# The stick-breaking product with the values: four stationary blocks of weights with 64 value columns streamed, and outputs turned back

## The chip, the cores and the metric

The kernel runs on one core of a Trainium2 chip. The metric is device time in microseconds of one execution, as the median of several runs. One profiled execution gives the trace from which rows are read here. PE is TensorE's matmuls, PEld its loads of the stationary operand, DVE VectorE, ACT ScalarE, POOL GpSimd, SP the engine that issues most DMAs.

## What is computed

One layer of a hybrid trunk on 1040 tokens (16 meta tokens and 1024 inputs) of width 1024. The normed input is projected; eight heads of 64 go through an RWKV-7 scan, eight through stick-breaking attention; both are joined and projected, and an FFN of width 4096 follows. All is float32. The attention is what the change touches:

```python
def stick_breaking_group(q, k, v, out_gain):
    for q0, q1 in bounds:
        z = jnp.einsum('bhqd,bhkd->bhqk', qb, kb) * scale
        mask = s_idx[None, :] < t_idx[:, None]
        log_beta = jax.nn.log_sigmoid(z)
        log_1m = jnp.where(mask, log_beta - z, 0.0)
        log_a = log_beta + lax.cumsum(log_1m, axis=3, reverse=True) - log_1m
        A = jnp.where(mask, jnp.exp(log_a), 0.0)
        outs.append(jnp.einsum('bhqk,bhkd->bhqd', A, vb))
    o = jnp.concatenate(outs, axis=2)
    o = o * lax.rsqrt(jnp.mean(jnp.square(o), axis=-1, keepdims=True) + RMS_EPS)
```

## The kernel before

The kernel is a row of stages, each a block in which every engine has its own program and engines meet by semaphores: the norm and turning of the input, the input projection with the preparation of the scan, the mixing stage (`stage_mix`), the head norms, the output projection, and the FFN. The change lies in `stage_mix` alone, which runs from about 389 to 919 us.

`stage_mix` computes the scan and the attention side by side. The scan works in 17 chunks of 64 tokens, all four head pairs at once, in 64x64 products (`each`, `crossed`, `doubled`, `three`), of which each waits for a copy or a sum by ACT or DVE of the product before. A chunk is cut into 8 steps of a front and 8 of a rear; a lap does the front of one chunk beside the rear of the chunk before, and there are 18 laps.

The attention ("sticks") is a pipeline over tasks. A task is one pair `i` (of 4), one head `h` of it, one group `g` of 512 queries and one block `b` of 128 keys: 112 tasks, of which the ones at the diagonal are 128, 256 or 384 queries wide and the other 64 are 512 wide. Scores and probabilities lie with keys on partitions and queries along the free axis. `sb_ticks` writes the tasks in a row, one to a tick, with three `Turn` ticks for each pair between them, in which PE transposes blocks of values (`vt`) and ACT copies them to `v`. A task is spread over eight ticks. At its tick PE computes the scores `zb` from `ks`, `qh` and `ql`; one tick later ACT copies them to `z` and DVE clamps them to `w`; then come exponential and logarithm on ACT, a maximum on DVE, and a split into `wsh` and `wsl` on POOL. Four ticks later PE multiplies by the triangle `tri` into `cb` (the running sum), DVE forms the exponent in `a` (L1121), five ticks later PE adds the other triangle `rest` to `cb`, which it may do only when DVE has read `cb`, and ACT makes `a` to weights (L1017). Six ticks later PE multiplies with the values into the PSUM bank `ob` (L1290); after the last key block of a unit ACT copies the head's 64 rows of `ob` to `o_sb` (L999, named `mixed_o` in rows).

In the product of L1290 the values of both heads of the pair, 128 columns, are the stationary operand, and `a` moves, up to 512 columns; half of the 128 output rows belong to the other head and are not used. `o_sb` so receives channels on partitions and tokens along the free axis, which is how the later stages read it. All operands of this product are plain float32; of each such matmul the trace has two load rows and two matmul rows. The products with `tri_r`, `rest_r`, `qh` and `ql` are in a rounded type (fp32r) and have one row each.

`program` sets how both are mixed: it walks through 18 x 8 places of the scan and after each gives out quarter ticks of the sticks, so many that they are evenly dealt: 4 x (124 + 7 + 1) = 528 quarters over 144 places. On PE the quarters of a tick are: scores or transposes, `rest`, `tri`, values. Each engine executes its list strictly in this order.

## Time and profile before

| | us |
|---|---|
| median of three runs | 1801.07 (1801.05 to 1801.92) |
| the profiled execution's own time | 1802.92 |
| its span, first to last instruction | 1801.0 |
| mixing stage, 389 to 919 us of the span | 530.2 |
| PE busy in it | 498.1 |

A row of a timeline is start in us from the span's start, length in us, engine, line, operation, output and inputs by the program's names (first the operand that moves, then the stationary one), sizes, and how many instructions are merged into it. In brackets stands idle time of the engine before it and who ended it. A matmul's length is from its start until its result stands, so matmuls in a row overlap: of several merged ones, the length of all less the length of one, divided by their number less one, is how far apart they start. For loads of the stationary operand the same holds.

### The profile page before, as it was taken

What the parts mean: (1) busy time and instruction counts of PE and PEld (TensorE: products, weight loads), DVE (VectorE), ACT (ScalarE), POOL (GpSimd) and SP (SyncE); (2) the same over time, 40 slices, a digit from 0 to 9 for tenths busy, and PEclk for the clock granted to TensorE, in tenths of its full rate; (3) what the DMA queues carried; (4) which work ended last, traced back from release to release, by engine and by line L of the source; (5) the groups of instructions that cost most, each with busy time, mean ns of one, the idle gap of its engine ahead of it and who ended that gap; (6) DMA issues with size and microseconds to landing.
All of it is one profiled execution on the core that took longest, in us unless ns stands there. A gap on an engine that the chain in (4) does not pass through costs nothing. (4 is left out here: it accounts for less than half of the span.)

```text
span 1801.0 us, 36214 instructions
## 1 busy us (share of the span) xinstructions
PE 1671.0 (93%) x14676; PEld 1389.2 (77%) x14676; DVE 825.3 (46%) x1125; ACT 698.6 (39%) x1222; POOL 508.5 (28%) x523
## 2 busy tenths in 40 slices
PE   4999999969999998999983987999999999999998
PEld 4999999957777776777742876888888888888886
DVE  5132432426555556555565443444444444444436
ACT  5253443426566565666571443122212211221112
POOL 6332532404434434344452433111111111111110
PEclk7999999979999999999996998999999999999999
DMA  3235266283202213110022213111111111111104
GB/s 140 109 121 183 97 204 208 93 208 93 65 25 72 53 48 77 26 40 23 23 94 82 93 71 124 64 47 47 47 47 50 54 47 47 47 47 47 48 22 164
DMA packets 79386, 143.84 MB, mean 80 GB/s; under 512 B 15505, under 2 KB 51345, under 8 KB 79265
## 3 DMA queue, kind: packets, MB, share of 16 engines
q1 hardware_dynamic: 75520, 128.26, 23.1%
q10 hardware_dynamic: 3744, 13.85, 1.9%
q8 instruction: 91, 1.49, 0.3%
q14 instruction: 31, 0.25, 0.0%
HBM read 104.51 MB, written 37.57 MB: 79 GB/s over the span
## 5 line engine op out<-in xcount | busy, mean ns | idle before, releaser
L1749 POOL TENSOR_TENSOR ffn_ul<-ffn_relu,ffn_uh 128x512 fp32r<-128x512 f32 x64 | 82.9, 1296 | 576.5 <-ACT ffn_uh L1721 576.5
L1778 DVE TENSOR_TENSOR all_acc<-all_acc,ffn_down 128x512 f32<-128x512 f32 x240 | 161.0, 684 | 122.0 <-PE ffn_down L1825 121.4
L618 PE MATMUL inproj_acc<-xn_xh,inproj_wh 128*128 128x346 f32 (+1 forms) x624 | 207.5, 333 | 8.4 <-DVE inproj_wl L539 8.4
L1817 PE MATMUL ffn_up<-all_mh,ffn_wuh 128*128 128x512 f32 x512 | 200.3, 391 | 11.9 <-DVE ffn_wul L1761 11.9
L618 PE MATMUL inproj_acc<-xn_xh,inproj_wl 128*128 128x346 f32 (+1 forms) x624 | 201.2, 322 | 0.0
L618 PE MATMUL inproj_acc<-xn_xl,inproj_wh 128*128 128x346 f32 (+1 forms) x624 | 201.0, 322 | 0.0
L1817 PE MATMUL ffn_up<-all_ml,ffn_wuh 128*128 128x512 f32 x512 | 200.1, 391 | 0.0
L1817 PE MATMUL ffn_up<-all_mh,ffn_wul 128*128 128x512 f32 x512 | 200.0, 391 | 0.0
L1825 PE MATMUL ffn_down<-ffn_wdh,ffn_uh 128*128 128x512 f32 x512 | 199.8, 390 | 0.0
L1825 PE MATMUL ffn_down<-ffn_wdh,ffn_ul 128*128 128x512 f32 x512 | 199.4, 389 | 0.0
L1825 PE MATMUL ffn_down<-ffn_wdl,ffn_uh 128*128 128x512 f32 x512 | 199.2, 389 | 0.0
L1769 DVE TENSOR_TENSOR ffn_relu<-ffn_relu 128x512 f32<-128x512 f32 x64 | 44.3, 692 | 219.9 <-ACT ffn_relu L1719 219.9
L1713 ACT ACTIVATE ffn_wdh<-ffn_raw_d 128x1024 fp32r<-128x1024 f32 x32 | 32.2, 1052 | 266.1 <-PE ffn_down L1825 265.2
L618 PEld LDWEIGHTS inproj_acc<-xn_xh,inproj_wh 128*128 128x128 f32 x624 | 117.9, 189 | 12.1 <-ACT inproj_wh L472 8.8
L1817 PEld LDWEIGHTS ffn_up<-all_mh,ffn_wuh 128*128 128x128 f32 x512 | 96.7, 189 | 32.5 <-DVE ffn_wul L1761 12.3
L618 PEld LDWEIGHTS inproj_acc<-xn_xl,inproj_wh 128*128 128x128 f32 x624 | 118.0, 189 | 3.3 <-issue 1.9
L618 PEld LDWEIGHTS inproj_acc<-xn_xh,inproj_wl 128*128 128x128 f32 x624 | 118.0, 189 | 0.0
L1719 ACT ACTIVATE ffn_relu<-ffn_up 128x512 f32<-128x512 f32 x64 | 38.3, 599 | 203.9 <-PE ffn_up L1817 203.9
L912 POOL TENSOR_TENSOR mix_wsl<-mix_w,mix_wsh 128x512 fp32r<-128x512 f32 (+1 forms) x96 | 113.3, 1180 | 8.1
L1825 PEld LDWEIGHTS ffn_down<-ffn_wdh,ffn_uh 128*128 128x128 f32 x512 | 96.1, 188 | 22.1 <-DVE all_acc L1778 2.6
L1817 PEld LDWEIGHTS ffn_up<-all_mh,ffn_wul 128*128 128x128 f32 x512 | 96.7, 189 | 20.3
L1817 PEld LDWEIGHTS ffn_up<-all_ml,ffn_wuh 128*128 128x128 f32 x512 | 96.7, 189 | 20.0
(250 smaller groups left out, 3460.4 us busy)
## 6 DMA issues: line engine op xcount, KB each, us to landing
ffn_raw_u<-in_w_up SPq DMA_DIRECT2D x32, 512.0 KB, 3.5
ffn_raw_d<-in_w_down SPq DMA_DIRECT2D x32, 512.0 KB, 4.3
xn_raw<-in_w_in SPq DMA_DIRECT2D x28, 512.0 KB, 4.5
p_scratch<-inproj_out ACTq DMA_DIRECT2D x26, 520.0 KB, 2.7
chunk_scratch<-inproj_fields SPq DMA_DIRECT2D x4, 2720.0 KB, 9.2
mix_swp<-chunk_scratch SPq DMA_DIRECT2D x68, 128.0 KB, 3.6
inproj_rkv<-p_scratch SPq DMA_DIRECT2D x14, 520.0 KB, 4.5
mix_fld<-chunk_scratch SPq DMA_DIRECT2D x17, 256.0 KB, 3.0
```

The source lines that it names most:

```text
L618: last = pe.matmul(acc[g][:, 0:size], w[s][:, kt, :], xx[:, kt, col:col + size], start=(kt == 0 and j == 0), stop=(kt == KD - 1 and j == 2))
L912: pool.tensor_tensor(low, part, high.bitcast(F32), ALU.subtract).then_inc(soft_low.sem, 1)
L1713: act.activation(wdh[s][:, f, :], raw_d[f][:, :], ACT.Copy).then_inc(wd_high.sem, 1)
L1719: act.activation(relu[j % 2][:, :], ups[j][:, :], ACT.Relu).then_inc(relu_done.sem, 1)
L1749: pool.tensor_tensor(ul[s][:, f, cols], relu[j % 2][:, :], uh[s][:, f, cols].bitcast(F32), ALU.subtract).then_inc(u_low.sem, 1)
L1769: dve.tensor_tensor(relu[j % 2][:, :], relu[j % 2][:, :], relu[j % 2][:, :], ALU.mult).then_inc(squared.sem, 1)
L1778: dve.tensor_tensor(part, part, downs[o % 4][:, :], ALU.add).then_inc(added.sem, 1)
L1817: last = pe.matmul(ups[j][:, :], w[f][:, k, :], xx[:, k, cols], start=(k == 0 and jj == 0), stop=(k == KD - 1 and jj == 2))
L1825: last = pe.matmul(downs[o % 4][:, :], u[s][:, f, t * P:(t + 1) * P], w[s][:, f, g * 512:g * 512 + 512], start=(first and f == 0 and jj == ...
```

## The change

The product with the values exchanges its operands. `a` is now stationary, one 128x128 block at a time (128 keys by 128 queries), and the head's 64 value columns move. A 512-wide task takes four such products, a 384-wide one three, and so on: 352 in all instead of 112. Their outputs have queries on partitions: `ob[:, j*64:(j+1)*64]` holds query block `j`. The output copy on ACT takes 256 columns instead of 512 (in blocks of 64, written with a stride so that both heads of a pair stand beside each other in `o_sb`), on all 128 partitions instead of 64.

Since later stages want channels on partitions, a new kind of tick, `Back`, does four 128x128 transposes from `o_sb` into a score bank `zb` on PE, and ACT copies the bank back over the same part of `o_sb`. There are eight, one for each pair and group. Six stand among the tasks of the next pair (before its 6th and its 11th task), two at the end with empty ticks before them, which take the place of the seven ticks of run-out. The row of ticks becomes 139 long, and 4 x 140 = 560 quarters are dealt over the same 144 places.

```diff
+BACK_BEFORE = {5: 1, 10: 0}
...
+                    if n in BACK_BEFORE and i:
+                        ticks.append(Back(i - 1, BACK_BEFORE[n]))
                     ticks.append(Task(i, h, g, b))
                     n += 1
-    return ticks
+    return ticks + [None] * 3 + [Back(PAIRS - 1, 1)] + [None] * 4 + [Back(PAIRS - 1, 0)]
...
-            quarters = 4 * (N + SB_LAG + 1)
+            quarters = 4 * (N + 1)
...
+                    if is_back(t):
+                        z_done.wait(act, t)
+                        act.activation(o_sb[:, at(t).i, at(t).g * SBW:(at(t).g + 1) * SBW], zb[t % 2][:, :], ACT.Copy).then_inc(z_copied.sem, 1)
                     yield
...
-                        act.activation(o_sb[half, i, g * SBW:(g + 1) * SBW], ob[half, :], ACT.Copy).then_inc(o_copied.sem, 1)
+                        act.activation(o_sb[:, i, g * SBW:(g + 1) * SBW].rearrange("p (j n) -> p j n", n=P)[:, :, half],
+                                       ob[:, 0:SBW // 2].rearrange("p (j n) -> p j n", n=HD), ACT.Copy).then_inc(o_copied.sem, 1)
...
+                    if is_back(t):
+                        i, g = at(t).i, at(t).g
+                        o_copied.wait(pe, outputs(i, g))
+                        for j in range(SBW // P):
+                            last = pe.transpose(zb[t % 2][:, j * P:(j + 1) * P],
+                                                o_sb[:, i, g * SBW + j * P:g * SBW + (j + 1) * P], ident[:, :])
                         last.then_inc(z_done.sem, 1)
...
-                        pe.matmul(ob[:, off:], v[i % 2][:, b, :], a[t % 3][:, off:], start=first, stop=at(t).last,
-                                  skip_group_check=True).then_inc(pv_done.sem, 1)
+                        for j in range(off // P, SBW // P):
+                            last = pe.matmul(ob[:, j * HD:(j + 1) * HD], a[t % 3][:, j * P:(j + 1) * P], v[i % 2][:, b, at(t).half],
+                                             start=(first and j == off // P), stop=at(t).last, skip_group_check=True)
+                        last.then_inc(pv_done.sem, 1)
```

Since the quarters are dealt anew, instructions move against the scan's steps on every engine. Two places on PE show it. In the names a number is the buffer; `mix_bank` products are the scan's.

The first place is the task with `wsh1` early in the stage, between its product with `tri` and its product with `rest`. Before:

```order
L1244 MATMUL mix_cb<-mix_wsh1,mix_tri_r 128x512
L1245 MATMUL mix_cb<-mix_wsl1,mix_tri_r 128x512
L1136 MATMUL mix_bank<-mix_zi8,mix_xx8 64x64 x8
L1136 MATMUL mix_bank<-mix_xx8,mix_zi8 64x64 x8
L1290 MATMUL mix_ob<-mix_a1,mix_v0 128x512
L1259 MATMUL mix_zb0<-mix_qh,mix_ks 128x384
L1259 MATMUL mix_zb0<-mix_ql,mix_ks 128x384
L1244 MATMUL mix_cb<-mix_wsh1,mix_rest_r 128x512
```

and now, on the same engine at the same task:

```order
L1261 MATMUL mix_cb<-mix_wsh1,mix_tri_r 128x512
L1262 MATMUL mix_cb<-mix_wsl1,mix_tri_r 128x512
L1315 MATMUL mix_ob<-mix_v0,mix_a1 128x64 x4
L1276 MATMUL mix_zb0<-mix_qh,mix_ks 128x384
L1276 MATMUL mix_zb0<-mix_ql,mix_ks 128x384
L1261 MATMUL mix_cb<-mix_wsh1,mix_rest_r 128x512
L1262 MATMUL mix_cb<-mix_wsl1,mix_rest_r 128x512
L1153 MATMUL mix_bank<-mix_zi8,mix_xx8 64x64 x8
```

The scan's doubling step, which stood between `tri` and `rest`, stands behind `rest` now. Stretches of `tri`, values, scores and `rest` with no scan step inside are 12 in the order before and 19 in the new one.

The second place is PE's last lap, from the last `tri` on. Before:

```order
L1244 MATMUL mix_cb<-mix_wsh3,mix_tri_r 128x512
L1245 MATMUL mix_cb<-mix_wsl3,mix_tri_r 128x512
L1290 MATMUL mix_ob<-mix_a1,mix_v1 128x384
L1136 MATMUL mix_bank<-mix_fv0,mix_xt 64x128 x8
L1290 MATMUL mix_ob<-mix_a2,mix_v1 128x512
L1136 MATMUL mix_bank<-mix_nb0,mix_wu 64x128 x8
L1290 MATMUL mix_ob<-mix_a0,mix_v1 128x512
L1232 MATMUL mix_bank<-mix_wu,mix_nb0 64x64 x2
```

and now:

```order
L1261 MATMUL mix_cb<-mix_wsh1,mix_tri_r 128x512
L1262 MATMUL mix_cb<-mix_wsl1,mix_tri_r 128x512
L1315 MATMUL mix_ob<-mix_v1,mix_a1 128x64 x3
L1153 MATMUL mix_bank<-mix_xx32,mix_nb0 64x64 x8
L1315 MATMUL mix_ob<-mix_v1,mix_a2 128x64 x4
L1153 MATMUL mix_bank<-mix_xx32,mix_zi32 64x64 x8
L1315 MATMUL mix_ob<-mix_v1,mix_a0 128x64 x4
L1153 MATMUL mix_bank<-mix_fv0,mix_xt 64x128 x8
L1153 MATMUL mix_bank<-mix_nb0,mix_wu 64x128 x8
L1249 MATMUL mix_bank<-mix_wu,mix_nb0 64x64 x2
```

The last two products with the values moved in front of the scan's last three steps; behind the last scan product now stand the four transposes of the last `Back`.

## Rows read from the trace of the kernel before

**Rows 1.** The page: busy us of each engine, share of the span, instructions.

```profile
PE 1671.0 (93%) x14676; PEld 1389.2 (77%) x14676; DVE 825.3 (46%) x1125; ACT 698.6 (39%) x1222; POOL 508.5 (28%) x523
```

**Rows 2.** Stretches: length, busy us of PE, PEld, DVE, ACT, POOL; clock; DMA.

```profile
389.00:919.20 530.20, 498.14 (x9027) 387.32 (x9023) 293.80 (x556) 316.45 (x645) 207.99 (x320) 0.99 0.22 51
389.00:407.20 18.20, 14.87 (x259) 11.79 (x255) 7.29 (x14) 7.41 (x16) 0.35 (x1) 0.76 0.76 149
407.20:919.20 512.00, 483.27 (x8770) 375.53 (x8769) 286.52 (x542) 309.04 (x631) 207.63 (x319) 1.00 0.20 48
```

**Rows 3.** TensorE in order of time: matmuls and loads, merged and single.

```profile
576.67 1.02 PE L1290 MATMUL mix_ob<-mix_a,mix_v 128*128 128x512 f32 x2
...
559.55 0.59 PE L1290 MATMUL mix_ob<-mix_a,mix_v 128*128 128x512 f32 x1
...
576.35 0.30 PEld L1246 LDWEIGHTS mix_cb<-mix_w,mix_tri 128*128 128x128 f32 x2 [0.17 <-issue]
...
576.35 0.19 PEld L1246 LDWEIGHTS mix_cb<-mix_w,mix_tri 128*128 128x128 f32 x1 [0.17 <-issue]
...
905.12 0.38 PE L1290 MATMUL mix_ob<-mix_a,mix_v 128*128 128x128 f32 x2
...
577.77 0.27 PE L1246 MATMUL mix_cb<-mix_w,mix_rest 128*128 128x128 f32 x1
```

**Rows 4.** Waits in the stage: who for whom, us in total, times, longest.

```profile
PEld mix_cb L1244 <- DVE mix_a L1121: 29.3, 33, 2.0
...
PE mix_ob L1290 <- ACT mixed_o L999: 2.1, 5, 0.6
```

**Rows 5.** Transposes in order of time, ns min/median/max, and stretches with clock.

```profile
6.74 1.03 PE L167 MATMUL pre_tp<-all_ident,pre_xs 16*128 16x16 f32 x8 [6.74 <-DVE pre_xs L146]
...
10.70 2.34 PE L167 MATMUL pre_tp<-all_ident,pre_xs 128*128 128x128 f32 x10
...
1047.72 1.04 PE L1604 MATMUL oproj_tp<-all_ident,oproj_t 128*128 128x128 f32 x8
...
L167 PE MATMUL pre_tp<-all_ident,pre_xs x72: 262/421/477, 6.7 to 30.1; 128*128 128x128 f32 x64, 16*128 16x16 f32 x8
...
L1604 PE MATMUL oproj_tp<-all_ident,oproj_t x64: 270/273/477, 1000.2 to 1080.1; 128*128 128x128 f32 x64
...
20.19:22.16 1.97, 1.97 (x8) 1.57 (x8) 1.97 (x2) 1.89 (x5) 1.97 (x1) 0.50 0.00 0
1047.72:1048.80 1.08, 1.08 (x10) 1.06 (x9) 0.00 (x0) 0.89 (x1) 1.08 (x1) 1.00 0.00 0
```

**Rows 6.** Loads: ns min/median/max of a line; busy us and mean ns.

```profile
L1290 PEld LDWEIGHTS mix_ob<-mix_a,mix_v x224: 186/188/193, 416.3 to 914.1; 128*128 128x128 f32 x112
...
L1604 PEld LDWEIGHTS oproj_tp<-all_ident,oproj_t x64: 138/141/231, 1000.0 to 1079.8; 128*128 128x128 f32 x64
...
L1136 PEld LDWEIGHTS mix_bank<-mix_xx,mix_zi 64*64 64x64 f32 x1360 | 46.0, 136 | 0.3 <-issue 0.3
```

**Rows 7.** ACT's groups in the stage: count, busy us, mean ns, idle before.

```profile
L936 ACT ACTIVATE mix_nb<-mix_bank 128x512 f32<-128x512 f32 x17 | 10.1, 595 | 11.7 <-PE mix_bank L1145 11.6
...
L999 ACT ACTIVATE mixed_o<-mix_ob 64x512 f32<-64x512 f32 x16 | 9.4, 588 | 0.7 <-PE mix_ob L1290 0.5
...
L965 ACT ACTIVATE mixed_y<-mix_bank 128x256 f32<-128x256 f32 x17 | 6.5, 384 | 53.7 <-PE mix_bank L1232 53.7
```

**Rows 8.** The last lap in order of time: ACT, DVE, scan loads.

```profile
912.07 0.60 ACT L961 ACTIVATE mix_wu<-mix_bank 128x512 f32<-128x512 f32 x1 [1.90 <-PE mix_bank L1136]
...
918.55 0.59 ACT L999 ACTIVATE mixed_o<-mix_ob 64x512 f32<-64x512 f32 x1
...
914.14 0.69 DVE L1078 TENSOR_TENSOR mix_qm<-mix_bank,mix_fld 128x512 f32<-128x512 f32 x1 [3.06 <-PE mix_bank L1136]
...
913.00 0.85 PEld L1136 LDWEIGHTS mix_bank<-mix_nb,mix_wu 64*64 64x64 f32 x16 [0.76 <-ACT mix_wu L961]
...
915.08 0.20 PEld L1232 LDWEIGHTS mix_bank<-mix_wu,mix_nb 64*64 64x64 f32 x4 [0.76 <-DVE mix_qm L1078]
```

More of the change, by code:

```diff
@@ L693, in __init__ @@
         self.i, self.part = i, part
+class Back:
+    def __init__(self, i, g):
+        self.i, self.g = i, g
 def sb_ticks():
@@ L733, in stage_mix @@
     is_turn = lambda t: isinstance(at(t), Turn)
+    is_back = lambda t: isinstance(at(t), Back)
     task_ticks = [t for t in range(N) if is_task(t)]
@@ L736, in stage_mix @@
     last_ticks = [t for t in task_ticks if ticks[t].last]
+    back_at = {(ticks[t].i, ticks[t].g): t for t in range(N) if is_back(t)}
+    outputs = lambda i, g: max(t for t in last_ticks if (ticks[t].i, ticks[t].g) == (i, g))
     of_head = {(i, h): [t for t in task_ticks if (ticks[t].i, ticks[t].h) == (i, h)] for i in range(PAIRS) for h in range(2)}
@@ L801, in stage_mix @@
         split_no = lambda i, h: 2 * i + h
-        z_done, z_copied = (Marks(m.sem(name), range(N)) for name in ("z_done", "z_copied"))
+        z_done, z_copied = (Marks(m.sem(name), [t for t in range(N) if ticks[t]]) for name in ("z_done", "z_copied"))
         (clamped, exp_done, ln_done, soft, soft_high, soft_low, tri_done, exponent, rest_done, weights, pv_done) = (
@@ L893, in before_diagonal @@
                                    pattern=[[1, P]], channel_multiplier=-1).then_inc(marks.sem, 1)
-            for now in range(N + SB_LAG):
+            for now in range(N):
                 t = now - 5
@@ L979, in sticks @@
                 high_k(0, 0)
-                for now in range(N + SB_LAG + 1):
+                for now in range(N + 1):
                     t = now - 1
@@ L1096, in sticks @@
                 low_k(0, 0)
-                for now in range(N + SB_LAG + 1):
+                for now in range(N + 1):
                     t = now - 1
@@ L1248, in sticks @@
             def sticks():
-                for now in range(N + SB_LAG + 1):
+                for now in range(N + 1):
                     t = now
```

1 line of the change is left out of this document (added).

## The prediction

> **What bounds the kernel now.** I read the page first (busy shares, then the slices), then the mixing stage as one window, then who waits there for whom, and last single instructions of TensorE in order of time. The page gives TensorE (PE) 1671.0 of 1801.0 us [rows 1], and the change touches only the mixing stage, 389 to 919 us. There PE is busy 498.1 of 530.2 us, while DVE has 293.8, ACT 316.5 and GpSimd (POOL) 208.0 [rows 2]. A busy PE isn't a full one here: a matmul's row is longer than what it costs when others follow. So the price of a matmul is read from starts. A product of probabilities and values, 128x512 in plain fp32, leaves two matmul records and two weight loads. Two records together last 1.02 us and one lasts 0.59 [rows 3], so the second starts 0.43 after the first, and the product costs 2 x 0.43 = 0.86 us. What is over in the stage goes to waits: PE's products with the `rest` triangle wait 29.3 us in 33 places for the DVE's exponent `mix_a` [rows 4]. No other named wait of PE is large. I therefore take PE's stream as the bound, with short waits on DVE in it, and pass each us of PE work on to the end in full.
>
> **The product itself.** It goes from moving 512 columns over one stationary block of values to four blocks of probabilities, stationary, each with 64 columns moving. The streaming falls: 0.43 us for 512 columns is 0.84 ns a column, so 64 columns stream in 0.054 us a record, half of it saved for a block. But each record brings a weight load of 128 columns, and what a load costs shows where it has nothing to hide behind: at 576.35 us two loads in a row last 0.30 together and 0.19 alone, so they start 0.11 apart [rows 3]. The 128-column products say the same: two records last 0.38, one 0.27, again 0.11 apart [rows 3]. There load and stream are of equal length, so this doesn't yet say which of them sets the pace when the stream is short. One place of the kernel does. Right at the start eight transposes with 128 columns loaded and only 16 moving last 1.03 us together, one 0.26, so they are 0.11 apart; a moment later ten with 128 moving last 2.34, one 0.42, so 0.21 apart [rows 5]. At a granted clock of 0.50, the 1.2 GHz level, eight take 1.97, so 0.22 apart, and at 1.00, the 2.4 GHz level, 1.04, with 0.27 for one, so 0.11 [rows 5]. The start of the kernel thus ran at the lower level, and there an eighth of the stream only halves the step: the load sets the pace and the matmul hides under it. At full clock such a load would be 0.055 us; a transpose's load row is 141 ns long and one of plain fp32 188 [rows 6], 0.05 more, which again makes 0.11 for the product's.
>
> So a block is 2 x 0.109 = 0.218 us and a full product 4 x 0.218 = 0.872, against 0.864 before; with 352 blocks (44 per head and pair, times 8) that is +0.9 us. Against it, a scan product behind it loads 64 columns only (136 ns against 188 [rows 6]), so it can start some 0.05 us sooner once the last short stream is over. In the new order 27 of the 112 products have such a follower: -1.4 us. Sum of the term: **-0.5 us**. No row has 128 plain fp32 columns loaded with 64 moving, so I bound it from both sides: at the transposes' one-pass 0.055 a load, 352 x 2 x 0.055 = -39 us, and if loads and streams didn't overlap, 352 x 2 x 0.053 = +37 us. I take the value near zero, since the rows of this very product give 0.11.
>
> The Trainium skill, "TensorE: Matmul & The Clock Gate", section "LDWEIGHTS (loading the stationary operand)", gives columns / 1.2 ns, so 107 ns here, and agrees. Its section "Back-to-back issue gap" gives about 81 ns a pair of load and matmul with 128 columns moving; by that the term would be near -20 us.
>
> **The transposes.** Eight new ticks of four 128x128 transposes each, 32 in all, turn finished outputs back. Eight in a row at full clock last 1.04 us, one 0.27 [rows 5], so 0.11 each: 32 x 0.11 = **+3.5 us** of PE. Bounds: 0, if they all fall into waits for the exponent, and 32 x 0.27 = 8.6 if each stood alone.
>
> The same page, section "PE-mode transpose", gives some 275 ns for one, 8.8 us for 32. The trace's duration agrees (0.27); by the start distance it isn't what a row of them costs.
>
> **ACT.** The 16 copies of finished outputs (588 ns each [rows 7]) become 128x256, which take 384 ns on the same engine out of PSUM [rows 7]: -3.3 us. Eight copies of 128x512 come (595 ns, as `mix_nb` [rows 7]): +4.8 us. ACT has 214 us free in the stage [rows 2], so +1.5 us there costs nothing by itself; if that cover were gone it would cost those 1.5. PE waited 2.1 us in 5 places for the output copy [rows 4]; it gets a third shorter, and I book **-1.0 us** (bounds -2.1 and 0). The back copies sit where a tick's score copy would be, before the exponentials of ACT's queue: 0.6 us behind which `mix_w` waits, and through it DVE.
>
> **The order.** Six of the ticks lie inside, and the row of ticks grows from 132 to 140 over the same 144 places of the scan, so between two scan steps there are 3.9 quarter ticks instead of 3.7. What hides the DVE's exponent between tri and rest is whatever PE has in between. Counted from both orders: stretches tri, values, score, rest with no scan step inside go from 12 to 19 (the stretch around task 1 in the order above is one of them). Such a place costs a wait of 0.89 us on the average (29.3 / 33 [rows 4]), at most +6 us. But only 12 of the 33 waits can lie there, and the other patterns with thin cover get rarer; all with under 1.5 us of cover go from 27 to 29, which is 2 x 0.89. I take **+2 us**, bounds -4 and +6.
>
> **The first and the last lap.** The last task's product stood at the end; now it ends one and a half places sooner. In the last lap two full products lay between the scan's steps: one while ACT copied `mix_wu` (912.07 to 912.67), one while DVE made `mix_qm` (914.14 to 914.83) [rows 8]. Both go up front, where they cost their 2 x 0.86. What is left behind is not two gaps closed: the next scan product can start at about 912.7 instead of 913.00 and the following at 914.9 instead of 915.08 [rows 8], so 0.5 us comes back and 1.2 stays: **+1.2 us**. At the very end stood the copy of `mixed_y` and behind it the output copy, 918.55 for 0.59 [rows 8]. Now the last transposes run under the copy of `mixed_y` (4 x 0.11 plus 0.2 till the result stands, against 0.38) and a copy of equal length follows: +0.2 us. The first lap waits for data and can take a little more of the denser row: -0.4 us.
>
> **Sum.** -0.5 + 3.5 - 1.0 + 2.0 + 1.2 + 0.2 - 0.4 = +5.0, of which I let 0.6 vanish, since a transpose before a rest product also covers its wait: +4.4 us. The profiled execution took 1802.92 us, its span 1801.0, 1.9 us more than the median 1801.07 of the runs; the sum moves it to 1807.3 and the median to **1805.5 us**. So the halved stream buys nothing, since loads take its place, and the turning back costs a little.
>
> **Rivals.** Cheaper loads (the other side): if a load of `mix_a` costs less when little streams beside it, the product wins. It decides at 0.103 us a load, where 704 x 0.006 give back the 4.4. At the one-pass rate of 0.055 it is 38 us less, 1767; halfway between both rates, 0.082, it is 19 less, 1786. For it speaks that all loads seen at 0.11 had as long a stream beside them; against it that the first of the two at 576.35 had none to wait for [rows 3]. The skill's 81 ns a pair, named above, is this rival's rule. Order gives back: the re-dealt places cover more waits than before (-4 instead of +2), 1799.5; no row forbids it. Loads bare: stream and load add, 1843; the 16-column transposes speak against it. The clock falls: granted 1.00 through the stage from 407 us [rows 2], with 0.43 us of streaming a record in the products; where waits broke the stream (389 to 407 us) it was 0.76 [rows 2]. If thinner streaming let it go to its lower level for some 50 us, up to 40 us more. That the change doesn't do what it says is no case: 64 columns do stream.
>
> **Chances.** The sum, with +1 to +9 us: 0.58 (0.36 of it beyond +3.6, 0.22 below). Order gives back: 0.24 (0.16 within 3.6 us of before, 0.08 further down). Cheaper loads: 0.10. Bare loads: 0.05. Clock: 0.03. About 0.2%, 3.6 us, is what a measurement of this kernel can tell from no change. Faster is 0.18, same 0.38, slower 0.44. The range goes from 1795 (order at its better bound, with transposes half hidden) to 1816 (order +6, transposes 8.6, the values' term +1); outside it lie the 0.18 of loads and clock.
>
> **What the changed profile would show.** The values' product: loads 0.109 apart, eight of them 0.87 us, half as much PE time in its matmul rows. Transposes of `mixed_o` 0.11 apart. The wait of rest products for `mix_a` at 29 to 36 us. In the last lap gaps of about 0.6 us before the last two scan products. The stage 4 to 5 us longer, all others as they were. I am wrong if loads start 0.06 or 0.16 apart, or if the stage gets shorter with loads at 0.109, which would mean that the order alone decides.

## The result

The changed kernel took 1806.75 us in the median of 7 runs (1806.48 to 1808.37); the kernel before, run beside it, 1801.05 (7 runs, 1799.5 to 1801.92). The ratio is 1.0036, 95% interval 1.0024 to 1.0047: 0.4% slower, 6.5 us, where the prediction had +4.4 and a range up to 1816. The profiled execution of the changed kernel took 1808.37 us with a span of 1806.5; that of before 1802.92 and 1801.0. Later batches gave medians of 1800.31 to 1801.46 for the kernel before (15 to 27 runs each). Every ratio below is to the kernel before in the same batch, so ratios can be set side by side across batches, and medians only with a us of doubt.

**The profile after.** First the page's busy times: us, share of the span, instructions.

```profile
PE 1677.2 (93%) x15188; PEld 1438.8 (80%) x15188; DVE 827.6 (46%) x1125; ACT 698.1 (39%) x1230; POOL 507.4 (28%) x523
```

Against [rows 1] PE has 6.2 us more and PEld 49.6 more, for 512 more instructions on each: 704 of the new product instead of 224, and 32 transposes. Now stretches of the mixing stage: length; busy us and instructions of PE, PEld, DVE, ACT, POOL; granted clock; DMA. The first answers to the first of [rows 2].

```profile
389.00:926.30 537.30, 506.32 (x9559) 438.56 (x9552) 295.77 (x556) 316.25 (x653) 208.27 (x320) 0.98 0.22 51
...
413.80:417.00 3.20, 3.20 (x51) 2.89 (x44) 1.02 (x2) 2.21 (x6) 0.21 (x1) 0.50 0.03 8
417.20:693.40 276.20, 262.59 (x5012) 227.47 (x5010) 164.61 (x298) 168.35 (x346) 115.40 (x174) 1.00 0.26 63
693.80:700.20 6.40, 6.21 (x72) 4.73 (x72) 1.65 (x4) 3.35 (x7) 1.87 (x2) 0.50 0.01 3
700.60:926.30 225.70, 213.33 (x4059) 186.25 (x4053) 116.58 (x229) 131.05 (x274) 87.08 (x136) 1.00 0.13 32
```

The stage ran from 387.9 to 926.6 us (538.7, from its first matmul to the head norms' first), where it had run from 386.9 to 919.4 (532.5): 6.2 us longer. It also began 1.0 us later, and the rest of the kernel behind it was 1.7 us shorter; both vary so in other runs here without any cause in the code (in fourteen profiled executions the stage begins at 386.0 to 387.9 us, and 879.5 to 881.6 us follow it). So the stage carries the whole loss, as forecast. What was not forecast is in the second and fourth row: twice the granted clock stands at 0.50, the 1.2 GHz level, in the middle of the stage. In the kernel before it was 1.00 from 407.2 us to the end of the stage [rows 2].

The named waits that answer to [rows 4] (waiting engine and its instruction, who released it; us, times, longest):

```profile
PEld mix_cb L1261 <- DVE mix_a L1138: 28.5, 30, 4.0
...
PEld mix_cb L1263 <- DVE mix_a L1138: 4.5, 4, 2.1
...
PE mix_ob L1315 <- ACT mixed_o L1015: 0.3, 1, 0.3
```

The sum for `mix_a` in the first row hardly moved (29.3 before, 28.5 now), but its longest member went from 2.0 to 4.0 us. The wait for the output copy went from 2.1 us in 5 places to 0.3 in one.

The first two of these rows, and the first of [rows 4], are idle time of PEld, which loads while PE still works; what costs time is the idle time of PE itself. Its rows for `mix_a` and `mix_krk`, before:

```profile
PE mix_cb L1244 <- DVE mix_a L1121: 18.3, 25, 1.6
PE mix_bank L1145 <- DVE mix_krk L1042: 4.0, 5, 1.4
...
PE mix_cb L1246 <- DVE mix_a L1121: 1.1, 3, 0.6
```

and now:

```profile
PE mix_cb L1261 <- DVE mix_a L1138: 20.0, 24, 3.7
PE mix_cb L1263 <- DVE mix_a L1138: 3.4, 4, 1.6
...
PE mix_bank L1162 <- DVE mix_krk L1059: 1.3, 3, 0.7
...
PE mix_bank L1162 <- DVE mix_a L1138: 0.6, 1, 0.6
```

On PE the waits for `mix_a` rose from 19.4 to 24.0 us, and those for `mix_krk` fell from 4.0 to 1.3. All its waits of over 0.15 us in the stage behind 401 us sum to 27.8 us before and to 27.0 now: on balance PE doesn't wait longer in the changed kernel.

**The product** is what the prediction said it would be: eight products of 64 columns, with their loads.

```profile
895.96 1.00 PE L1315 MATMUL mix_ob<-mix_v,mix_a 128*128 128x64 f32 x8
...
895.74 1.08 PEld L1315 LDWEIGHTS mix_ob<-mix_v,mix_a 128*128 128x128 f32 x8
...
896.74 0.19 PEld L1276 LDWEIGHTS mix_zb<-mix_qh,mix_ks 128*128 128x128 f32 x1
```

The first load starts at 895.74 and the load that follows the eight at 896.74; a load row is 0.19 long, so the last of the eight started at 895.74 + 1.08 - 0.19 = 896.63, and the load behind it 0.11 later. Over all 352 pairs in the trace the median distance from load to load is 0.112 us. Forecast was 0.109.

**The transposes** and the last lap, in order of time:

```profile
912.98 0.65 PE L1290 MATMUL mix_zb<-all_ident,mixed_o 128*128 128x128 f32 x4
...
920.19 1.09 PE L1153 MATMUL mix_bank<-mix_nb,mix_wu 64*64 64x128 f32 x16 [0.70 <-ACT mix_wu L974]
922.07 0.33 PE L1249 MATMUL mix_bank<-mix_wu,mix_nb 64*64 64x64 f32 x4 [0.79 <-DVE mix_qm L1095]
...
925.02 0.66 PE L1290 MATMUL mix_zb<-all_ident,mixed_o 128*128 128x128 f32 x4
...
925.71 0.60 ACT L1009 ACTIVATE mixed_o<-mix_zb 128x512 f32<-128x512 f32 x1 [0.19 <-PE mix_zb L1290]
```

One transpose's row is 0.273 us long in the median of the 32, so four in 0.65 are 0.125 apart. The two gaps of the last lap (0.70 and 0.79) now stand open, where full products stood in them before; forecast was about 0.6 each.

**Where the 6.2 us arose.** A lap is read from the start of its first `mix_bank<-mix_fld` product with 128 columns moving (407.20 for lap 1 before, 408.35 after) to the next lap's. Lap 0 begins with the stage; the last entry holds the last two of the 18 laps, up to the end of the stage's last product. Lengths in us, and the difference:

```
lap      0     1     2     3     4     5     6     7     8     9    10    11    12    13    14    15    16
before 20.27 31.67 31.51 28.34 28.92 32.44 30.25 29.39 29.63 28.73 34.71 30.46 30.16 29.72 34.17 30.56 50.25
after  20.43 36.75 30.53 29.13 28.39 33.47 30.94 29.59 28.87 30.72 36.10 30.91 29.07 28.82 33.20 31.07 49.76
diff   +0.16 +5.08 -0.98 +0.79 -0.53 +1.03 +0.69 +0.20 -0.76 +1.99 +1.39 +0.45 -1.09 -0.90 -0.97 +0.51 -0.49
```

The differences sum to +6.6; measured to the head norms' first product the last entry is 51.6 and 50.7 (-0.9), and they sum to the 6.2. They have both signs: that is the order at work, which deals TensorE's instructions anew. The product and the transposes alone could not shorten lap 12 by a us or lengthen lap 1 by five; e2 below, which has neither, has laps 1 and 12 at 35.73 and 29.03.

### The profile page after: what moved, and what is told of

Same layout as the page of the kernel before. It is cut to its first block and busy times, and to the rows that moved or that the text cites. A ratio compares the mean times of both kernels' runs of the same rounds, so it can differ in the third digit from the quotient of the medians.

```text
span 1806.5 us, 37254 instructions
## 1 busy us (share of the span) xinstructions
PE 1677.2 (93%) x15188; PEld 1438.8 (80%) x15188; DVE 827.6 (46%) x1125; ACT 698.1 (39%) x1230; POOL 507.4 (28%) x523
## 3 DMA queue, kind: packets, MB, share of 16 engines
q8 instruction: 95, 1.56, 0.4%
```

## Experiments

There were twelve, in four batches. The first (e1 to e4) takes the change apart; the second (e5 to e8) and third (e9 to e11) test what the order does; e12 came last.

**e1: the product alone.** The kernel before with the new product and the new output copy, without ticks, order and transposes of the change.

```diff
-                        pe.matmul(ob[:, off:], v[i % 2][:, b, :], a[t % 3][:, off:], ...)
+                        for j in range(off // P, SBW // P):
+                            last = pe.matmul(ob[:, j * HD:(j + 1) * HD], a[t % 3][:, j * P:(j + 1) * P], v[i % 2][:, b, at(t).half], ...)
...
-                        act.activation(o_sb[half, i, g * SBW:(g + 1) * SBW], ob[half, :], ACT.Copy)
+                        act.activation(o_sb[:, i, ...].rearrange("p (j n) -> p j n", n=P)[:, :, half], ob[:, 0:SBW // 2]..., ACT.Copy)
```

> The kernel before with the new product alone: four stationary blocks of weights, 64 value columns moving, output copy of 256 columns. No turning back, no new ticks: the order of all else is that of before. Its attention output stays unturned. Theory A (the sum of the prediction): loads pace the product at 0.112 us as in the changed kernel's trace, 704 x 0.112 = 78.8 us against about 76 before, less what followers and the shorter output copy give: +0 to +2 us against before, granted clock 1.00 throughout the stage. Theory B (the clock): thinner streaming lets the clock fall for one or more stretches inside the stage, as at 413.7 and 693.6 us of the changed kernel: +3 to +6 us, with falls in this trace too. Theory C (the order and the transposes cost all of it): 0, no fall of the clock.

Measured: 1799.58 us (11 runs), ratio 0.9996 (0.9987 to 1.0005), so -0.7 us with -2.3 to +0.9. Halving the streamed columns is worth nothing that can be measured. Cheaper loads (-19 or -38 us) and bare loads (+37) are out. The time fits theories A and C. But A had the clock at 1.00 throughout, and the profiled execution has one stretch at 0.50, from 846.1 to 849.5 us, behind a wait of 1.44 us; the lap with it took 31.97 us against 30.56 before. So such a stretch isn't peculiar to the changed kernel, and B's +3 to +6 us is out all the same.

**e2: the order alone.** The old product and copy, the new row of ticks, with empty ticks where the `Back` ticks stand.

```diff
-                        ticks.append(Back(i - 1, BACK_BEFORE[n]))
+                        ticks.append(None)
...
-    return ticks + [None] * 3 + [Back(PAIRS - 1, 1)] + [None] * 4 + [Back(PAIRS - 1, 0)]
+    return ticks + [None] * 9
```

> The old product and the old output copy, but the row of 139 ticks of the changed kernel with empty ticks where the eight Back ticks stand, so 560 quarters over the 144 places and no transposes. Theory A: +2 for the order, +1.2 for the last lap, -0.4 for the first: about +3 us against before, clock 1.00. Theory B (the clock does it): 0 to +1. Theory C (order alone decides): +5 to +6, the whole of the change's cost.

Measured: 1805.79 us, ratio 1.0031 (1.0019 to 1.0042), +5.6 us. That is theory C's number (+5 to +6) and not A's +3: the same work in another order costs almost as much as the whole change.

**e3: the order and the transposes, with the old product.** e2 with its `Back` ticks live.

```diff
-                        for j in range(off // P, SBW // P):
-                            last = pe.matmul(ob[:, j * HD:(j + 1) * HD], a[t % 3][:, j * P:(j + 1) * P], v[i % 2][:, b, at(t).half], ...)
+                        pe.matmul(ob[:, off:], v[i % 2][:, b, :], a[t % 3][:, off:], ...)
```

> As the one before, with the eight Back ticks live: transposes and copies are made, but the product is the old one, so its outputs end up turned. Theory A: 3 us more than the order alone (32 x 0.11 less what hides), about +6 against before. Theory B: no fall of the clock here, since the product streams 512 columns: +3 or less, and the step from here to the changed kernel is +3 or more. Theory C: the same as the order alone.

Measured: 1809.32 us, ratio 1.0054 (1.0040 to 1.0068). Against e2 the medians give +3.5 for the transposes, as A had it; against e3 the changed kernel with its new product is at -2.6 (the two ran in different batches; by ratios -3.2). The clock fell in the profiled executions of e2 and e3 too, twice in each, with the product streaming its full 512 columns, where theory B had no fall in e3.

**e4: the new product with all 128 value columns moving.** Same loads, twice the stream.

```diff
-                            last = pe.matmul(ob[:, j * HD:(j + 1) * HD], a[t % 3][:, j * P:(j + 1) * P], v[i % 2][:, b, at(t).half], ...)
+                            last = pe.matmul(ob[:, j * P:(j + 1) * P], a[t % 3][:, j * P:(j + 1) * P], v[i % 2][:, b, :], ...)
```

> The changed kernel with all 128 value columns moving past each stationary block, as before, instead of 64; the output copy picks the head's half. Loads are the same 704, streams twice as long (0.107 us a record). If loads set the pace, each record stays at about 0.11 us and the time is that of the changed kernel within 1 us. Theory B: the array streams as much as before, so the clock doesn't fall inside the stage, and it is 3 us or more faster than the changed kernel, though it streams more. If streams counted (loads cheaper than 0.1 us), it would be slower than the changed kernel by several us.

Measured: 1808.50 us, ratio 1.0049 (1.0035 to 1.0063); 1.75 us over the changed kernel by medians (2.3 by ratios), for 704 records with twice the columns. "Within 1 us" was expected; the intervals leave that open, and e4's runs also had the lower mean clock (0.968 against 0.969, see behind e12). The row of e4 that answers to the one at 895.96 above:

```profile
897.16 1.05 PE L1315 MATMUL mix_ob<-mix_v,mix_a 128*128 128x128 f32 x8
```

Eight take 1.05 instead of 1.00 us, and the 0.05 is the longer stream of the last. Loads stand 0.112 apart as before. So the load of 128 plain fp32 columns sets the pace, and the stream hides beneath it at 64 columns as at 128. The clock stood at 0.50 in this kernel too, at nearly the same places and once more (412.5 to 415.9, 692.4 to 699.2, 825.5 to 829.0), so it isn't the thinness of the stream that lets it fall.

**The row on which the rest turns.** In e2 lap 10 holds TensorE's longest wait. TensorE there:

```profile
685.50 1.12 PE L1313 MATMUL mix_ob<-mix_a,mix_v 128*128 128x512 f32 x2
690.83 0.79 PE L1260 MATMUL mix_cb<-mix_wsh,mix_rest_r 128*128 128x512 f32 x1 [4.21 <-DVE mix_a L1137]
```

and DVE in the same stretch, every row:

```profile
684.96 2.31 DVE L1108 TENSOR_TENSOR mix_ks<-mix_k,mix_ks 64x1152 fp32r<-64x1152 f32 x1
687.30 0.69 DVE L1130 TENSOR_TENSOR mix_w<-mix_z,mix_w 128x512 f32<-128x512 f32 x1
687.91 0.68 DVE L1055 TENSOR_TENSOR mix_nb<-mix_bank,early_masks 128x512 f32<-128x512 f32 x1
688.51 0.43 DVE L1057 COPY_PREDICATED mix_xx<-early_masks,mix_bank 128x256 f32<-128x256 uint32 x1
688.84 0.68 DVE L1058 TENSOR_TENSOR mix_krk<-mix_bank,early_masks 128x512 f32<-128x512 f32 x1
689.44 0.43 DVE L1060 COPY_PREDICATED mix_xx<-early_masks,mix_bank 128x256 f32<-128x256 uint32 x1
689.77 0.43 DVE L1083 COPY_PREDICATED mix_zi<-early_masks,mix_bank 128x256 f32<-128x256 uint32 x1
690.10 0.68 DVE L1137 TENSOR_TENSOR mix_a<-mix_z,mix_cb 128x512 f32<-128x512 f32 x1
```

DVE executes its list in order. The low part of the next head's keys (`mix_ks`, 2.31 us: the split that `split_at` places eight ticks ahead of a head's first task), the maximum and five operations of the scan's front all stand ahead of the exponent `mix_a`, for which the `rest` product waits, and TensorE has no scan step to do meanwhile. At 820 us in e2 stands a similar place (2.56 us), and the granted clock is at 0.50 behind both (690.6 to 694.0, 820.3 to 823.7). The changed kernel has the place in lap 10 at 693.99, with 3.74 us of waiting (its rows stand under e9). The kernel before has the split there too, but the scan's front stands ahead of it and TensorE's scan steps run beside it, so the wait is shorter:

```profile
684.36 1.35 DVE L1092 TENSOR_TENSOR mix_ks<-mix_k,mix_ks 64x1152 fp32r<-64x1152 f32 x1
...
687.09 0.50 PE L1244 MATMUL mix_cb<-mix_wsh,mix_rest_r 128*128 128x512 f32 x1 [1.56 <-DVE mix_a L1121]
```

The same `mix_ks` took 1.35 us there and 2.31 in e2, and the rows of POOL show why. In e2 POOL had begun a `mix_wsl` just before:

```profile
684.73 1.33 POOL L925 TENSOR_TENSOR mix_wsl<-mix_w,mix_wsh 128x512 fp32r<-128x512 f32 x1
```

It ended at 686.06, and `mix_ks` 1.21 us later. In the fourteen traces 50 splits (`mix_ks` or `mix_ql`) start while a `mix_wsl` runs; each ends 1.21 to 1.22 us (`mix_ks`) or 1.08 to 1.09 us (`mix_ql`) behind the end of that `mix_wsl`, and they last 1.38 to 2.33 us. The 117 that start while POOL does nothing last 1.35 to 1.36 and 1.21 to 1.22. So 1 us of e2's wait is a second collision, of DVE with POOL, which the order before did not have at this place.

So here is theory D: what the order costs comes from places where a split and the scan's front meet ahead of an exponent. Its rival, E, was for e5 to e8 that the cost is spread over many thin places, and for e9 to e11 that such a wait is only moved about, so that what one lap gives back the next takes.

**e5, e6, e8: the split twelve ticks ahead instead of eight**, for every head, in the changed kernel (e5), the kernel before (e6) and e2 (e8). The edit moves ACT's part of the split (`mix_qh` and the upper part of `mix_ks`) along with DVE's; no run separates the two.

```diff
-    split_at = {of_head[i, h][0] - 8: (i, h) for i, h in of_head if (i, h) != (0, 0)}
+    split_at = {of_head[i, h][0] - 12: (i, h) for i, h in of_head if (i, h) != (0, 0)}
```

> The changed kernel with the preparation of a head's queries and keys (ACT's mix_qh and mix_ks, DVE's mix_ql and mix_ks) twelve ticks ahead of the head instead of eight. Nothing else moves. Theory D (formed from the order-only run): the order's cost sits in a few places where DVE has the 2.3 us sum for mix_ks and the scan's five front operations in its queue ahead of the exponent, so that PE waits up to 5 us and the clock falls behind it. Those before 691 and 820 us vanish with their falls of the clock: 2 to 4 us less than the changed kernel, 1803 to 1805. Theory E (the cost is spread over many thin places): within 1 us of the changed kernel.

> The kernel before with the same shift from eight to twelve ticks. Theory D: it too has waits of about 2 us at 624, 717, 808 and 847 us behind such preparations, so it gets 1 to 3 us faster. Theory E: 0 within 1 us.

> The order-only kernel with the preparation twelve ticks ahead. Theory D: the waits of 5.2 and 3.6 us at 691 and 820 us and the two falls of the clock go, and most of the 5.5 us over before with them: +1 to +3 against before. Theory E: stays at +5.

Measured: e5 1806.81 us, ratio 1.0033 (1.0021 to 1.0045), no change against the changed kernel; e6 1799.27, 0.9991 (0.9982 to 1.0000); e8 1808.21, 1.0035 (1.0021 to 1.0049). e6 gained 1.6 to 2.2 us, as theory D had it. e5 and e8 gained nothing, where D had 1803 to 1805 us and +1 to +3, so by these two totals it would have fallen. The laps say otherwise. Of the changed kernel with lead 8 and with lead 12 (e5):

```
lap      0     1     2     3     4     5     6     7     8     9    10    11    12    13    14    15    16
lead 8 20.43 36.75 30.53 29.13 28.39 33.47 30.94 29.59 28.87 30.72 36.10 30.91 29.07 28.82 33.20 31.07 49.76
lead12 20.55 38.35 30.53 30.25 28.39 35.94 30.90 30.96 28.86 31.09 31.11 30.92 28.30 28.85 31.59 31.07 49.77
```

Laps 10, 12 and 14 give 5.0, 0.8 and 1.6 us, as D wants; laps 1, 3, 5 and 7 take 1.6, 1.1, 2.5 and 1.4, while laps 2, 4, 6 and 8 between them are the same to 0.04 us, so nothing is passed on from lap to lap. The losses are new meetings of the same kind, for other heads. The worst in e5, TensorE:

```profile
413.85 0.79 PE L1263 MATMUL mix_cb<-mix_w,mix_rest 128*128 128x128 f32 x2 [4.12 <-DVE mix_a L1138]
```

and DVE before it:

```profile
409.47 1.35 DVE L1109 TENSOR_TENSOR mix_ks<-mix_k,mix_ks 64x1152 fp32r<-64x1152 f32 x1
...
413.52 0.28 DVE L1138 TENSOR_TENSOR mix_a<-mix_z,mix_cb 128x128 f32<-128x128 f32 x1
```

In the stretch from 412.8 to 419.2 the clock is at 0.50 in this kernel. A single lead for all heads can't be right; which lead is right depends on where a head begins in a lap.

**e7: the order with a shorter tail.** e2 with seven empty ticks at the end instead of nine, to see what the longer row of ticks costs.

```diff
-    return ticks + [None] * 9
+    return ticks + [None] * 7
```

> The order-only kernel (old product, empty ticks instead of Back) with seven empty ticks at the end instead of nine, as many as the run-out of before: the quarters are dealt for 138 ticks instead of 140, the six inner empty ticks stay. The prediction's last-lap term says the two more ticks cost about 1.2 us, so this should be 1 us or more faster than the order-only kernel (5.5 over before). If places of collision decide (theory D), it may go either way by some us, since all of them shift.

Measured: 1807.02 us, ratio 1.0030 (1.0018 to 1.0042). Nothing is won; but the quarters are dealt anew once more (lap 1 33.5 instead of 35.7, lap 16 55.2 instead of 49.4), and in its profiled execution, the slowest of the six, the clock was at 0.50 from 911.7 to 918.6 us, inside the tail. So this run doesn't isolate the tail, and it is taken only as a third order of the same work that costs some 5 us. It is inconclusive on the last lap.

**e9, e10, e11: a lead of twelve only where it helped.** The last three heads get it, in the changed kernel (e9), the kernel before (e10) and e2 (e11).

```diff
-    split_at = {of_head[i, h][0] - 8: (i, h) for i, h in of_head if (i, h) != (0, 0)}
+    split_at = {of_head[i, h][0] - (12 if (i, h) in ((2, 1), (3, 0), (3, 1)) else 8): (i, h)
+                for i, h in of_head if (i, h) != (0, 0)}
```

> The changed kernel, with the split of queries and keys moved from eight to twelve ticks ahead only for the last three heads (pair 2 second half, pair 3 both halves); the other four stay at eight. Theory D (a split step stands in DVE's queue ahead of the exponent mix_a; the wait that TensorE has there is what the new order costs): lap 10 falls from 36.1 to about 31 us, laps 12 and 14 by 0.8 and 1.6, laps 1 to 8 stay as in the changed kernel; the time is about 1800 us (1806.8 - 7 + 0.4), level with the kernel before. The fall of the granted clock at 693.6 to 700.4 us is gone. Theory E (zero sum: what one lap gives the next takes, since TensorE has the same work to do): laps 11, 13 and 15 get longer by as much, time about 1806.

> The kernel before with the same selective lead of twelve ticks for the last three heads. Theory D: laps 10 and 14 fall by 2.5 and 1.6 us as when all heads were moved, laps 1 to 9 keep their lengths; 1801.1 - 3.5 = about 1797.5 us, below both kernels. Theory E: 1801.

> The new order alone (old product, no turning back, the new ticks empty) with the same selective lead. Theory D: laps 10, 12 and 14 give 2.2, 0.7 and 3.1 us against the new order at a lead of eight, about 1800.5 us, so that the order as such costs nothing and only its collision with the splits did. Theory E: 1805.8 as without it.

Measured: e9 1799.58 us, ratio 0.9990 (0.9981 to 0.9999); e10 1796.48, 0.9980 (0.9971 to 0.9989); e11 1800.22, 0.9993 (0.9984 to 1.0002); 11 runs each. All three are within about 1 us of what theory D gave, and 4.5 to 6.4 from E. e9 is level with the kernel before or a little faster, 7 us below the changed kernel; e10 is the fastest kernel of this study. The place in lap 10, changed kernel first, TensorE and then DVE:

```profile
689.64 0.61 PE L1290 MATMUL mix_zb<-all_ident,mixed_o 128*128 128x128 f32 x4
693.99 0.80 PE L1261 MATMUL mix_cb<-mix_wsh,mix_rest_r 128*128 128x512 f32 x1 [3.74 <-DVE mix_a L1138]
...
700.33 0.87 PE L1153 MATMUL mix_bank<-mix_xx,mix_nb 64*64 64x64 f32 x22
```

```profile
688.11 2.31 DVE L1109 TENSOR_TENSOR mix_ks<-mix_k,mix_ks 64x1152 fp32r<-64x1152 f32 x1
690.46 0.69 DVE L1131 TENSOR_TENSOR mix_w<-mix_z,mix_w 128x512 f32<-128x512 f32 x1
...
693.25 0.68 DVE L1138 TENSOR_TENSOR mix_a<-mix_z,mix_cb 128x512 f32<-128x512 f32 x1
```

and the same instructions of e9:

```profile
686.41 0.61 PE L1290 MATMUL mix_zb<-all_ident,mixed_o 128*128 128x128 f32 x4
688.42 0.50 PE L1261 MATMUL mix_cb<-mix_wsh,mix_rest_r 128*128 128x512 f32 x1 [1.40 <-DVE mix_a L1138]
...
691.99 1.15 PE L1153 MATMUL mix_bank<-mix_xx,mix_nb 64*64 64x64 f32 x32
```

```profile
685.50 0.68 DVE L1056 TENSOR_TENSOR mix_nb<-mix_bank,early_masks 128x512 f32<-128x512 f32 x1
...
687.69 0.67 DVE L1138 TENSOR_TENSOR mix_a<-mix_z,mix_cb 128x512 f32<-128x512 f32 x1
```

These rows price both parts of the loss. The wait goes from 3.74 to 1.40: 2.3 us. And from the start of the `rest` product to that of the scan product further down are 6.34 us in the changed kernel (693.99 to 700.33, clock 0.50) and 3.57 in e9 (688.42 to 691.99, clock 1.00): 2.8 us more for the same instructions. Together 5.1; lap 10 fell from 36.10 to 31.22. The clock's share is the greater one.

In e9 no stretch of the stage behind 397.9 us is below 1.00:

```profile
397.90:920.00 522.10, 496.97 (x9444) 428.92 (x9444) 290.14 (x553) 316.53 (x652) 211.20 (x320) 1.00 0.20 50
```

But D in its strong form falls with the same batch. I had expected of e11 that the order as such costs nothing. Against e10, which has the same lead in the old order, e11 is 2.3 us slower by the ratios and 3.7 by the medians. The collisions at the splits were in the kernel before too, though shorter (e10 gains 3.6 to 4.7 us). So of the order's 5.6 us some 2 to 3 are longer collisions at the late splits, and the other half remains. The largest piece of that is lap 1: 31.67 in e10 and 35.74 in e11 (lap 9 adds 2.3). Some of lap 1's growth is work that the new order deals to it and takes from later laps (12 and 13 are 1.7 and 0.9 shorter in e11 than in e10). The rest, 2.4 us, are longer waits of PE for an exponent, which no split has to do with. Over the whole stage PE waits 17.6 us for `mix_a` in e10 and 22.5 in e11. The first two such waits of lap 1 in the changed kernel, DVE and then TensorE:

```profile
410.14 0.69 DVE L1056 TENSOR_TENSOR mix_nb<-mix_bank,early_masks 128x512 f32<-128x512 f32 x1
...
412.33 0.28 DVE L1138 TENSOR_TENSOR mix_a<-mix_z,mix_cb 128x128 f32<-128x128 f32 x1
...
418.83 1.23 DVE L1131 TENSOR_TENSOR mix_w<-mix_z,mix_w 128x512 f32<-128x512 f32 x1
```

```profile
412.67 0.49 PE L1263 MATMUL mix_cb<-mix_w,mix_rest 128*128 128x128 f32 x2 [1.64 <-DVE mix_a L1138]
...
420.58 0.44 PE L1261 MATMUL mix_cb<-mix_wsh,mix_rest_r 128*128 128x384 f32 x1 [0.91 <-DVE mix_a L1138]
```

The first stands behind the scan's front alone. The second stands behind a maximum, `mix_w`, of 1.23 us instead of 0.69: POOL's `mix_wsl` ran until 419.51. No run removed either.

**e12: the transposes with the old product, once more, with e9's lead.** e3 with the edit of e9.

> The changed kernel with the old product and the old output copy (the turned outputs' content is not the reference's), and with the selective lead of twelve ticks for the last three heads. It gives the two remaining terms again with the collisions gone: the transposes against the order alone under the same lead (1800.22), and the product against the changed kernel under the same lead (1799.58). If both terms are costs in TensorE's stream and nothing else, this run is at 1800.2 + 3.5 = about 1803.5, and the product is then worth 3 to 4 us less. If the product's gain of 2.6 us on top of the transposes came from the places of the waits at the splits, this run is at about 1800 to 1801 and the product is worth under 1 us.

Measured: 1803.64 us (11 runs), ratio 1.0014 (1.0005 to 1.0023). The transposes are +3.4 by medians against e11 (+3.8 by ratios), again as in the first pair; the product on top of them -4.1 against e9 (-4.3). So the first alternative in the expectation held.

The terms, by ratios times 1801, with the medians' differences beside them:

| term | lead 8 | lead 12 for three heads | forecast |
|---|---|---|---|
| order | e2: +5.6 (5.5) | e11 less e10: +2.3 (3.7) | +2.8 with both laps |
| transposes | e3 less e2: +4.1 (3.5) | e12 less e11: +3.8 (3.4) | +3.5, less 0.6 |
| product and its copy, alone | e1: -0.7 (-0.7) | | -1.5 |
| the same on top of both | after less e3: -3.2 (-2.6) | e9 less e12: -4.3 (-4.1) | -1.5 |
| whole change | +6.5 (5.7) | e9 less e10: +1.8 (3.1) | +4.4 |

Every ratio has an interval of 0.0009 to 0.0014 to either side, 1.6 to 2.5 us, so a difference of two is uncertain by 2 to 3.

Part of these differences goes with the clock. The mean granted clock of every execution is on record, to 0.001, which is about one stretch of 3.4 us at 0.50. Over 183 executions, each set against those of its own kernel and batch, 0.001 less goes with 1.2 us more (correlation -0.75). The mean over the runs is 0.9706 to 0.9710 for the kernel before, 0.9697 for e2, 0.9680 for e3, 0.9689 for the changed kernel, and 0.9705, 0.9705, 0.9696 and 0.9703 for e10, e11, e12 and e9. By this slope and the mean times, the order at lead 8 costs 4.0 us at equal clock instead of 5.6, and the transposes about 1.5 instead of 3.5 (2.3 instead of 3.3 at lead 12). It is a correlation, and why e3 had the lower clock it doesn't say; the rows of lap 10 show once, by the same instructions, how a stretch at 0.50 costs time.

## Why the prediction was right, and where not

**The product (-0.5 and -1.0 for its copy's wait).** Right in its reasons: loads are the pace, at 0.112 us for 0.109 forecast, which on 704 is 2 us more than booked (the booked +0.9 is 0.7 by its own numbers, 88 times 0.008); e4 shows the stream hidden, and the wait for the output copy fell by 1.8 of its 2.1 us. The rule of the Trainium skill, "TensorE: Matmul & The Clock Gate", section "Back-to-back issue gap", of some 81 ns a pair didn't hold for these loads: its result, near -20 us, is refuted by e1. The Trainium skill, "TensorE: Matmul & The Clock Gate", section "LDWEIGHTS (loading the stationary operand)", gives 107 ns for 128 columns, close to the 112 measured. Alone the two terms gave -0.7. On top of the transposes they gave 2.6 to 4.1, more than forecast. PE's waits in the stage, counted in the same way, account for much of it: 29.6 us in e3 against 27.0 in the changed kernel, 26.2 in e12 against 22.8 in e9, of which the wait for the output copy is 1.6 each time. The profiled executions of e12 and e9 differ in few laps: lap 9 by 1.28 us (in e12 PE waits 1.48 us at 673.69 for an exponent behind a `mix_w` that met POOL's `mix_wsl`, and in e9 it doesn't), lap 8 and 16 by 0.6 each, and laps 0 and 1 by 1.0 and 0.85, in both of which e12's clock stood longer at 0.50. Before lap 1 no product with the values has run, so at least that us is not the product's. One forecast by the way was wrong: the product's matmul rows don't halve. They sum to 94.1 us for 704, and in e2, with the old product, to 67.2 + 13.4 + 9.9 + 6.9 = 97.4 for 224, since a short record still lasts 0.27 us. Rows' lengths overlap and say nothing of what a product costs.

**The transposes (+3.5).** The term was measured at 3.5 and 3.4 us. But its reason is only half seen. I had summed 32 starts on TensorE's path. In the profiled executions of e2 and e3 the laps with the six inner `Back` ticks (two in lap 5, one each in 9, 10, 13 and 14) differ by -0.03, -0.05, +0.12, +0.35 and +0.01 us; lap 16, where the other two stand, is 0.95 longer (1.15 to the end of the stage), and the stage 537.7 instead of 536.4. There the inner transposes lie almost entirely in the waits for `mix_a`, which fall on PE from 22.2 + 4.3 to 21.0 + 3.4 us, and e3's profiled execution was the fastest of its five (1806.87, median 1809.32). Between e11 and e12, whose profiled executions are near their medians, lap 1 has +0.9 with a stretch at the lower clock that e11 lacks, lap 9 +1.4 and lap 16 +1.0. So the last two ticks cost 1.0 to 1.2 us. The other 2.5 of the median are in no trace, but the recorded clocks point to them: e3's profiled execution had 0.970, as e2's runs (0.969 to 0.970), and its other four had 0.967 or 0.968 and took 1.8 to 4.1 us longer. So most of the 2.5 goes with a lower clock, and the term's agreement with 3.5 is in good part luck.

**The order (+2.0, with -4 and +6 as bounds).** This is the step that was mis-sized: 5.6 us. Its mechanism was named rightly, waits for `mix_a` where no scan step stands between `tri` and `rest`, and the sum of PEld's waits came out as forecast: 28.5 + 4.5 us in the changed kernel against 29.3 in [rows 4], at 29 to 36 foreseen. But the prediction read that row as PE's own wait. On PE the waits for `mix_a` went from 19.4 to 27.2 us in e2 (22.2, 4.3 and 0.7), and the other waits gave 3.9 back (`mix_krk`, 4.0 before and 1.2 in e2, was among the waits called not large). All PE's waits in the stage behind 401 us are 27.8 us before and 31.7 in e2, and 23.1 and 27.0 in e10 and e11: the order brings 3.9 us of idle time at either lead, and in the changed kernel the transposes and the exchanged product fill it up again. Two things more were left out. First, every place was priced at one mean wait, 0.89 us of PEld's. A wait's length is set by what stands ahead of the exponent on DVE, and where a split and the scan's front stand there it was 3.74 and 4.21 us, 1 us of it because DVE's split met POOL's `mix_wsl`. I had counted what TensorE has between `tri` and `rest` and never what DVE and POOL have. Second, the clock. "Granted 1.00 through the stage" was read as a property of the stage; it held with waits for `mix_a` of 2.0 at the most [rows 4]. The two stretches at 0.50 hold 3.2 and 6.4 us of the rows shown above, and the longer one alone cost 2.8.

**The last lap (+1.2 and +0.2).** Not seen. The gaps stand where they were forecast, 0.70 and 0.79, but the lap with them is 0.5 us shorter than before, and 0.9 shorter in e2 (0.9 and 1.5 to the end of the stage). Presumably the two products moved to the front met waits there or in the two laps before; no run isolates it. The first lap, forecast at -0.4, was +0.16 here and -1.1 in e2; the short stretch at 0.50 at its start differs by 3.4 us in length between executions of kernels that don't differ there, and with it the lap by about a us, so neither sign means anything.

**The clock as a rival** (0.03, "thinner streaming"). A fall did happen, for another reason and by some tenth of the 40 us. e2, e3 and e4 show that the stream's width isn't it. In the traces 20 of the 21 stretches at 0.50 behind lap 0 begin in the last 1.5 us of a wait of PE for `mix_a` or within 1.5 us after it (lengths are PE's, as in the rows shown); the other, in e6 at 416.2, begins 2.3 us behind one of 1.03. Waits of 3.7 to 4.2 us were followed by one in all six kernels that had such a wait (the changed kernel, e2, e3, e4, e5, e8). Of those of 2.05 to 2.56 us five were (one each in e2, e3, e4, e5, e8) and two were not (2.11 at 824.70 in the changed kernel, 2.20 at 690.86 in e7). Shorter ones go both ways at the same instruction: 1.63 at 410.99 in e12 was followed by one, 1.63 at 410.09 in e9 not; e1 has one behind 1.44 at 845.60, and e6, with the old order and product, one behind 1.56 at 627.56. The kernel before, whose longest such wait on PE was 1.6, had none in its profiled execution. So longer waits make it likelier, and no bound can be read from these rows.

Altogether +6.5 measured against +4.4, with the order 2.8 over, the product on top of the rest 1 to 3 under and the transposes as forecast in size. The number was close because two of these misses offset each other, which is luck. The lower end of the range, 1795, doesn't follow from the two terms named for it, which give 1797.8 (1799.5 less half of 3.5).

## What to carry to other kernels

Where engines run fixed lists and one bounds the time, a change that deals the list anew can cost as much as what it adds. Price it place by place: for each wait of the bounding engine, count what the releasing engine has in its own queue ahead of the release, see whether a third engine holds that up, and look for the tail, not the mean. Read the wait on the engine that does the work, not on the one that loads for it. A wait of several us cost twice here, once as idle time and once in the clock behind it. And moving a long operation of the releaser (here a split of 1.4 to 2.3 us) out of the few places where it meets other work was worth more than the whole rewriting of the product; a uniform shift only changed which places it met. Halving what streams past a stationary block gains nothing once the load of that block is the pace.

## What the runs showed of the hardware

- A load of 128 stationary plain fp32 columns steps at 0.112 us at full clock, with 64 as with 128 columns streaming beside it (e4). Each of a product's two load rows pays it.
- A transpose's row is 0.273 us long and four in a row start 0.11 to 0.13 apart; in a wait they cost nothing in the traces (inner laps of e3 against e2).
- The granted clock fell to its lower level behind single waits of TensorE in the middle of dense work, each time where they were 3.7 to 4.2 us (six of six) and at times where they were shorter. The same instructions then took 6.34 instead of 3.57 us.
- The same DVE operation, `mix_ks` on 64x1152, took 2.31 us at 684.96 in e2 and 1.35 at 409.47 in e5. At the one place POOL was in the middle of a `mix_wsl`, at the other it did nothing; in 50 cases of 50 such a split ended a fixed time (1.21 or 1.08 us) behind the end of the `mix_wsl` that was running when it started.
